# The 256-column matmuls read their moving operand, and write PSUM, in another order of 64-byte lines

## What is computed

```python
for i in range(DEPTH):                      # DEPTH = 2
    x = x + 0.5 * swiglu(rmsnorm(x, norm_ff1[i]), ff1_w_gate[i], ff1_w_up[i], ff1_w_down[i])
    x = x + token_mixer(rmsnorm(x, norm_mix[i]), w_in[i], ...)      # attention, gated linear attention, W_out
    x = x + 0.5 * swiglu(rmsnorm(x, norm_ff2[i]), ff2_w_gate[i], ff2_w_up[i], ff2_w_down[i])
    g = jax.nn.sigmoid(rmsnorm(x, norm_ple[i]) @ ple_w_gate[i])
    x = x + g * (p[i] @ ple_w_proj[i])
return rmsnorm(x, norm_final)
# swiglu(h, g, u, d) = (silu(h @ g) * (h @ u)) @ d, with 2816 hidden features; w_in has 5720 columns
```

## Time and profile before

| what | value |
|---|---|
| median of 3 runs | 1246.23 us (1245.46 to 1246.38) |
| profiled execution, its own time | 1246.01 us |
| its span, first to last instruction | 1244.2 us |
| matmuls (PE) busy | 1216.6 us, 98% of the span, 10226 instructions |
| weight loads (PEld) busy | 1182.7 us, 95% |
| VectorE (DVE) busy | 810.8 us, 65% |
| ScalarE (ACT) busy | 599.2 us, 48% |
| mean granted TensorE clock | 0.990 of full |

### The profile page before, as it was taken

How to read it: one execution, slowest core, us unless ns; L and a number is a source line. 1 busy time by engine, 2 the same in 40 slices (tenths; PEclk the granted TensorE clock), 3 DMA queues, 4 the chain that set the end, 5 groups by cost and what they waited for, 6 DMA issues and landing times.

```text
span 1244.2 us, 23623 instructions
## 1 busy us (share of the span) xinstructions
PE 1216.6 (98%) x10226; PEld 1182.7 (95%) x10226; DVE 810.8 (65%) x924; ACT 599.2 (48%) x675; POOL 126.2 (10%) x137
## 2 busy tenths in 40 slices
PE   6999999999999999999999999999999999999997
PEld 6999999999889999999999999999899999999996
DVE  5666555687768666655756665548786676666554
ACT  6444444555644544444544444356456454444443
POOL 2000001002510100001200000100033120000011
PEclk8999999999999999999989999999999999999998
DMA  8555555353324555555355555554533355555540
GB/s 289 180 195 203 189 189 198 137 202 137 136 102 170 185 198 201 196 183 199 137 199 183 197 203 188 187 196 146 198 124 115 121 185 191 191 203 195 180 169 35
DMA packets 33736, 218.80 MB, mean 176 GB/s; under 512 B 5312, under 2 KB 5728, under 8 KB 7648
## 3 DMA queue, kind: packets, MB, share of 16 engines
q1 hardware_dynamic: 33632, 217.27, 49.1%
HBM read 216.21 MB, written 1.05 MB: 175 GB/s over the span
## 4 chain that ended last, share of the span: by engine, by line
PE 87%; DVE 6%; issue 2%; ACT 2%; DMA 1%; POOL 1%; SPq 0%; POOLq 0%; DVEq 0%; ACTq 0%
PE psum L355 27%; PE psum L356 27%; PE psum L357 27%; DVE w_lo L1089 2%; ACT w_hi L738 1%; PE psum L464 1%; PE psum L586 1%; PE psum L567 1%; DMA raw<-in_weights 1%; PE psum L611 1%; PE psum L615 0%; PE psum L552 0%; DVE dist L1245 0%; DMA x<-in_x 0%; DVE hB_lo L1417 0%
## 5 line engine op out<-in xcount | busy, mean ns | idle before, releaser
L1089 DVE TENSOR_TENSOR w_lo<-raw,w_hi 128x2048 fp32r<-128x2048 f32 x202 | 462.6, 2293 | 252.6 <-ACT w_hi L738 252.3
L738 ACT ACTIVATE w_hi<-raw 128x2048 fp32r<-128x2048 f32 x202 | 387.1, 1917 | 417.4 <-PE psum L357 408.5
L355 PE MATMUL psum<-hA_hi,w_hi 128*128 128x256 f32 x1376 | 383.9, 279 | 0.9 <-DVE gates L1136 0.9
L356 PE MATMUL psum<-hA_hi,w_lo 128*128 128x256 f32 x1376 | 380.1, 276 | 0.0
L357 PE MATMUL psum<-hA_lo,w_hi 128*128 128x256 f32 x1376 | 380.1, 276 | 0.0
L355 PEld LDWEIGHTS psum<-hA_hi,w_hi 128*128 128x128 f32 x1376 | 258.3, 188 | 5.4 <-issue 3.7
L356 PEld LDWEIGHTS psum<-hA_hi,w_lo 128*128 128x128 f32 x1376 | 258.4, 188 | 0.2
L357 PEld LDWEIGHTS psum<-hA_lo,w_hi 128*128 128x128 f32 x1376 | 258.3, 188 | 0.0
L355 PE MATMUL psum<-hB_hi,w_hi 128*128 128x256 f32 x832 | 234.8, 282 | 14.5 <-DVE w_lo L1489 7.4
L356 PE MATMUL psum<-hB_hi,w_lo 128*128 128x256 f32 x832 | 233.3, 280 | 0.0
L357 PE MATMUL psum<-hB_lo,w_hi 128*128 128x256 f32 x832 | 233.0, 280 | 0.0
(11 more groups left out here) (169 smaller groups left out, 1267.1 us busy)
## 6 DMA issues: line engine op xcount, KB each, us to landing
raw<-in_weights SPq DMA_DIRECT2D x203, 1024.0 KB, 4.8
x<-in_x SPq DMA_DIRECT2D x4, 256.0 KB, 5.0
raw<-in_weights SPq DMA_DIRECT2D x4, 256.0 KB, 5.4
out<-gates SPq DMA_DIRECT2D x4, 256.0 KB, 2.4
relu<-in_p SPq DMA_DIRECT2D x2, 256.0 KB, 5.5
consts<-in_consts SPq DMA_DIRECT2D x1, 448.0 KB, 10.7
gnorm<-in_gla_norm SPq DMA_DIRECT2D x2, 64.0 KB, 4.8
consts<-in_consts SPq DMA_DIRECT2D x1, 64.0 KB, 6.3
```

Of the source, the lines that this page charges most:

```text
L355: pe.matmul(o, lh, rh, start=start, stop=False)
L356: pe.matmul(o, ll, rh, start=False, stop=False)
L738: act.activation(w_hi[:, s, :], raw[:, s, :], ACT.Copy).then_inc(hi_ready[s], 1)
L1089: dve.tensor_tensor(w_lo[:, s, :], raw[:, s, :], w_hi[:, s, :].bitcast(F32), ALU.subtract).then_inc(lo_ready[s], 1)
```

## The change

The three tiles are still read whole, and each product is still three matmuls with the same weights. What changes is the order in which a matmul runs through the 256 columns of its moving operand, and, in the same order, through the 256 columns of its output. In units of one 64-byte line (16 columns), 0 to 15, the order was 0, 1, 2 ... 15 everywhere. Now it is:

- `hB`: 0, 8, 1, 9, 2, 10 ... 7, 15;
- `hA`: 0, 2, 4 ... 14, then 1, 3, 5 ... 15;
- `hid`: 0, 1, 8, 9, 2, 3, 10, 11 ... 6, 7, 14, 15.

`by_tokens`, `branch`, and the projection pass no order and stay as they were.

```diff
+            def halves_in_turn(t):
+                return t.rearrange("p (h j t) -> p j h t", h=2, t=16)
+
+            def even_then_odd(t):
+                return t.rearrange("p (j h t) -> p h j t", h=2, t=16)
+
+            def halves_by_two(t):
+                return t.rearrange("p (h j t) -> p j h t", h=2, t=32)
+
+            ORDER = {"hB": halves_in_turn, "hA": even_then_odd, "hid": halves_by_two}
+
-            def three(o, lh, ll, rh, rl, start, stop):
+            def three(o, lh, ll, rh, rl, start, stop, order=None):
 
+                if order is not None:
+                    o, rh, rl = (ORDER[order](t) for t in (o, rh, rl))
                 pe.matmul(o, lh, rh, start=start, stop=False)
                 pe.matmul(o, ll, rh, start=False, stop=False)
                 return pe.matmul(o, lh, rl, start=False, stop=stop)
...
                     for k in range(8):
                         mm = three(o[:, c * T:(c + 1) * T], wh[:, k, c * P:(c + 1) * P], wl[:, k, c * P:(c + 1) * P],
-                                   h[0][:, k, :], h[1][:, k, :], k == 0, k == 7)
+                                   h[0][:, k, :], h[1][:, k, :], k == 0, k == 7, "hA")
...
                     mm = three(bank[first + c][:, 0:T], wh[:, k, c * P:(c + 1) * P], wl[:, k, c * P:(c + 1) * P],
-                               h[0][:, k, :], h[1][:, k, :], k == 0, k == 7)
+                               h[0][:, k, :], h[1][:, k, :], k == 0, k == 7, "hB" if h is hB else "hA")
...
                             mm = three(bank[DOWN_BANKS[m] + i][:, 0:T], wh[:, u, i * P:(i + 1) * P], wl[:, u, i * P:(i + 1) * P],
-                                       hid[0][:, k, :], hid[1][:, k, :], k == 0, k == 21)
+                                       hid[0][:, k, :], hid[1][:, k, :], k == 0, k == 21, "hid")
```

## The result

The changed kernel takes 1306.43 us (median of 4 runs, 1304.69 to 1306.90) against 1246.31 for the kernel before (median of 4, 1245.46 to 1247.96): 1.0478 times as long, with a 95% interval of 1.0460 to 1.0496. The forecast was no change, and the time lies above the range.

A forecast was written before the change was run, and what follows sets the result against it. TensorE's matmuls were taken as the bound. Access pattern, SBUF order and PSUM order summed as 0 + 0 + 0 on the profiled 1246.01 us, so the median, 1246.2 us, was predicted; 8 in 10 range 1228 to 1300.

The forecast's parts named there:

- What bounds the kernel: Whole kernel: TensorE's matmuls, 8736 on the three tiles at 113.3 ns, 990 us or 80% of the span.
- The access pattern with more dimensions: Moving operands of the three tiles: breaks in the pattern cost 0, upper bound one more cycle for each run.
- the second rival: Three tiles: each run costs a cycle, 6.7 ns on hB and hA, 3.3 on hid; 51 us, 1297; chance 0.12.
- The group on which the 0 rested: Line 586's bursts: 1.60 us for 16 matmuls with single elements or runs of 32, read as breaks costing nothing.
- level 1: Line 586's burst whose moving operand is single elements 8 bytes apart; 1.60 us for 16 matmuls, as at level 6.
- The order of lines in SBUF: Moving reads of the three tiles: taken as 0, bounds for a tile from -4.3 to +6.7 ns.
- the prediction's two cases: Moving reads in SBUF: lines cost one cycle whichever comes next (113.3 ns), or the extra cycles come of meeting weight loads.
- the 120 ns after the restart: hA, 241.86 to 242.34 us: four steps at 120 ns before settling, used as the upper bound for a tile.
- The first rival: Three tiles: new orders never settle, 6.7 ns a matmul; one tile 1260 to 1274, all three 1305; chance 0.25.
- The order of lines in PSUM: Output of the three tiles' matmuls, written in whole 64-byte pieces: cost taken as 0.
- The faster rival: Three tiles: the extra 16 cycles were meetings; pitch falls towards 109 ns, hB alone 1235.5, all 1209; chance 0.23.
- the 109 ns of the earlier trace: Transposes moving 128 columns, some 109 ns apart: read as what the weight load allows, the lower bound for the pitch.

The follow-up runs named there:

- e4: Changed kernel with only 32 of 128 weight columns in the three tiles' matmuls, save the first and last product of a group: 1296.73 us.
- e15: Changed kernel with a single weight column in the three tiles' matmuls, save the first and last product of a group: 1295.26 us.
- e7: Changed kernel with hA in its old order, hB reading every second element within a line, hid within two lines, their outputs in a row: 1791.74 us.
- e3: Kernel before with only 32 of 128 weight columns in the three tiles' matmuls, save the first and last product of a group: 1243.30 us.
- e10: Kernel before with the three tiles 64 bytes further on against the weights (place 256 instead of 192): 1295.36 us.
- e13: Kernel before with the tiles 64 bytes further on and 32 of 128 weight columns, save the first and last product of a group: 1274.66 us.
- e1: Changed kernel with only the PSUM output in the new orders and the moving operand in SBUF read in a row: 1248.44 us.
- e6: Changed kernel with other run lengths: hB 4 runs of 64 columns, hA 8 of 32, hid 32 of 8 (its output in a row): 1285.44 us.
- e12: Changed kernel with hA back in its old order, hB and hid in the new ones: 1273.72 us, ratio 1.0219.

## Why the prediction was wrong

**What bounds the kernel** was read rightly: the matmuls, at full clock, and every nanosecond of pitch went to the end. No other engine's work changed, and the parts by pitch give 63.3 us where 60.1 were measured.

**The access pattern with more dimensions** is the step that failed. The prediction put: "I take 0, and keep as upper bound the price of one more cycle for each run". The truth lay at that upper bound. With one weight column the runs of 16 columns cost 6.7 ns (e4, e15) and those of 32 some 3.7, together 6624 x 6.7 + 2112 x 3.7 = 52 us, beside the 51 that the second rival gave. The group on which the 0 rested, was float32 of 64 columns at some 100 ns each, and the prediction itself said that such matmuls could hide a small cost. e7 shows how much it can be: single elements 8 bytes apart, the very pattern of level 1, make the float32r matmul of 256 columns take 240.0 ns for 113.3. So the row should have weighed next to nothing against a bound of 51 us. The matmuls at hand were the better guide: at a granted 1.00 they took 113.3 ns, 6 to 7 more than half of the 213 to 214 at 0.50, and e3 shows that this stays with 32 weight columns. That TensorE was already waiting for its moving read is my estimate from these; no run shows the wait itself.

**The order of lines in SBUF.** No row and no run shows the 0 that the sum has for this part; the runs showed 6.5 ns for `hB`, 8.7 for `hA` and 5.2 for `hid`. Of the prediction's two cases, that lines cost the same whichever comes next is refuted by them. That the reads can meet is shown by another place and not by the order: 119.1 ns with 128 weight columns and 113.3 with 32 (`hid`, e10 and e13). What the 120 ns after the restart in the earlier trace rows are is not shown; at the same restart in e3, with 32 weight columns from 242.17 us on, four steps from 241.94 to 242.40 take 0.46 us, 115 ns. The first rival took the loss for meetings with the weight load that never settle. A part of the loss does go with the weight load: 2.2 ns by 4128 for `hA` and 1.5 by 2112 for `hid`, 12 us in all. The three orders were ranked rightly, `hB` showing no such part. But it is the smaller part, and 120 ns in `hB` was not a meeting: it is the same with 128, 32 and 1 weight columns and at both places. The prediction's "113.3 is the same for three tiles and looks like a property of lines" was half right: no read in a row went faster, with narrow weights either (e3), but it is reached with whole weights at some places only, and 64 bytes away the old order itself costs 49.5 us more (e10).

**The order of lines in PSUM** at 0 was right (e1).

**The faster rival** was wrong in its mechanism: the 113.3 ns of the old order stay with 32 of 128 weight columns (e3), so they do not come down with the weight load, and the 109 ns of the earlier trace rows, read from other matmuls, was no goal. That it was the weight load that set those 109 was an estimate, which no run shows. No order or place tried has a lower pitch than the kernel before.

**The two rivals together.** The range ended at one cost for all tiles, 1297 rounded to 1300, and the chances took the rivals as alternatives. Both held, in their two parts, and their sum, 52 + 12 us less what idle time and the rest took up, lies outside. `hA` alone lost 8.7 ns, more than the 6.7 that the prediction took as the most for a tile. That the 1305 of the first rival on all three tiles, which was left out of the range, comes near the measured 1306 is chance: it had 6.7 ns everywhere, from meetings, and the runs show 6.5, 8.7 and 5.2, for the most part not from meetings.

What stays open: why four runs are free and why 32 cost less than a cycle each (both had whole weights in e6, and were not run with narrow ones), and why orders with as many runs differ by up to 3.5 ns. It is also not shown how one order at one place settles into one of two speeds, 117.8 or 119.3 ns, or why the old order at 192 settles into a state without meetings.

## What to carry to other kernels

When matmuls are the bound and their pitch at a granted 1.00 is above half of the one at 0.50, as 113.3 ns was here against half of 213 to 214, suspect the moving read, and try that operand in long runs: in float32r runs of 64 columns were free in the one order tried (113.5 ns), runs of 32 and 16 took 117.8 to 122.4 with whole weights, and the output's order did not matter (113.3 to 113.6 in e1). Do not take the price of a broken-up read from matmuls of another length and type: the 64-column ones of the earlier trace rows took 100 ns with single elements and with runs of 32. When two costs of a change have different causes, add them in the range, and don't only set them against each other. A pitch that is even in all tiles may still hang on where tiles start: move one by 64 bytes and look before calling it a floor (113.3 became 119.1 in e10).

## What the runs showed of the hardware

- A float32r moving operand of 256 columns, read in a row at the place 192, takes 113.3 ns at a granted 1.00, with 128 or with 32 weight columns beside it (before, e3). At 0.50 the changed kernel's `hB` takes 213 ns, like the old order: twelve matmuls from 20.78 to 23.12 are 2.34 us by 11.

```profile
20.78 0.41 PE L368 MATMUL psum<-hB_hi,w_hi 128*128 128x256 f32 x1
...
23.12 0.41 PE L370 MATMUL psum<-hB_lo,w_hi 128*128 128x256 f32 x1
```

  So at a granted 0.50 the breaks into runs of 16, which cost 6.7 ns at 1.00, cost nothing.
- Every second element of a moving float32r operand takes 240.0 ns for 256 columns, a bit more than a read in a row takes for twice as many (230 for 512 in the earlier trace rows), and 240 at a granted 0.50 too (e7). From 240.0 and 230 I estimate that such a read goes by the bytes passed over and not by the elements used; no run separates the two.
- Where a moving tile starts against the weights, modulo 512 bytes, is worth up to 5.8 ns of 113.3 on each matmul among the four places tried (192, 256, 320, 448): 256 instead of 192 makes the whole kernel 1.04 times as long (e10).
- The same order at the same places can run at two steady pitches, 117.8 and 119.3 ns, and it changed from the one to the other when only the matmuls before it read in another order (the changed kernel beside e12).
- Writing PSUM in broken-up runs of 16 or 32 columns costs nothing (e1: 113.4 ns beside a read in a row).
